# One transformer-like layer on one core: a software pipeline of three attention units instead of two, beside the delta-rule blocks, and one activation table for the normalisations behind it

## The chip, the cores and the metric

The kernel runs on one core of one Trainium2 chip. The metric is the device time of the program in microseconds. All arithmetic is float32 except two small masks.

## What is computed

The layer has DEPTH = 1, 1024 tokens and width 1024. The core of the reference:

```python
p     = x @ w_in
y_A   = rwkv7_time_mix(token_shift(p[:, A]))      # 6 heads x 64, delta-rule state, group norm per head
y_B   = rglru_mix(p[:, B])                        # 4 blocks x 64, gated linear scan
y_C   = stick_breaking_attention(p[:, C])         # 6 heads x 64, strictly causal
x     = layer_norm(ALPHA * x + concat(y_A, y_B, y_C) @ w_out)
x     = layer_norm(ALPHA * x + grouped_moe(x))    # 16 experts, top 2 of one group
...
z         = q @ k.T * scale                       # stick-breaking attention, one query block of 128
log_keep  = where(mask, log_sigmoid(-z), 0)
after     = reversed_cumsum(log_keep) - log_keep
attn      = where(mask, exp(log_sigmoid(z) + after), 0)
o         = head_rms_norm(attn @ v)
```

## The kernel before

**Stages.** TensorE first makes the projections (`proj_pe`, matmuls at L201 and L210), with the gated linear scan and the preparation of the delta rule on the other engines beside it. Then comes the stage that the change touches: 8 delta-rule blocks of 128 tokens (`mats_pe`, `mats_act`, `mats_dve`, `mats_pool`) side by side with the attention. Behind it, in `after_delta_pe`, `after_delta_act` and `after_delta_dve`, come the group norm of the delta rule (six items, `rnorm_*`), the output projection (`out_pe`, L1200), the first LayerNorm (`out_dve`, `out_norm_act`) and the router's logits. The router and the experts (L1677) follow.

**One block of the delta rule** has 13 steps (k = 0 to 12), written as a generator for each engine. Step 0 makes products (L689, L694), which VectorE masks (L811, L816, L805). Step 1 transposes rows (L701), ScalarE copies them (L775). Steps 2 to 10 build an inverse level by level: TensorE multiplies (L640), ScalarE copies a product (L779), VectorE updates two matrices under a mask (L805). Steps 11 and 12 make the block's results (L736, L748 and on), with copies at L795 and L798 and additions at L841 and L842. The state is carried by `state_pe` (L662, L665) and `state_dve` (L674, L675).

**The attention** has 36 units (`SPANS`): a pair of heads, 128 queries and up to 512 keys; 12 units to each pair of heads. A unit goes through: `Z` = q k on TensorE into `PS[0]` (L953, L957), two sigmoids on ScalarE, of -z into `E2` (L1003) and of z (L1007), a reversed running product on VectorE for each head (`sba_scan`, L1021), the weights (`sba_weights`, L1034, with L1031 for a carry), then for each head a transpose on TensorE into the one half of `PS[1]` (L970) and its copy by VectorE (L1043), and the product with v in two halves (L981), which ScalarE copies out (L994). Before the change two units are at work at once: the five pieces (`KINDS`) of number j belong to unit u = j // 5 for the front part and u - 1 for the transposes and the products with v.

**The order** is written out by hand. `side_by_side` runs the generator of a block on each engine, and issues `PIECES[k]` pieces of attention after step k; each engine runs its queue in this order, and semaphores carry the dependences.

```python
PIECES = [3, 2, 1, 2, 1, 2, 1, 2, 1, 2, 2, 2, 2]
for k, _ in enumerate(mats(e, b)):
    if b in SNORM_AT:
        snorm(e, SNORM_AT.index(b), k)
    for _ in range(PIECES[k]):
        piece(e, j)
```

**The head norm of the attention** (`snorm_*`) runs for each pair of heads: a square (L1059), the sum over heads on TensorE (`heads_sum`, L344, into `PS[0]` for the first two pairs), Ln (L1062) and Exp (L1064), and a multiplication on VectorE (L1087). For pairs 0 and 1 it stands in blocks 3 and 6, for pair 2 behind the last block. The next `Z` has to wait until Ln has read `PS[0]`. The tables of ScalarE are loaded where the compiler puts them, unless `exp_ln` (L240) names one that holds both Ln and Exp. The group norm's root is L899 and L901, its use L912, L914 and L917, its means L879 and L906, its gates L884 and L888; the LayerNorm has L1313, L1128 to L1138 on VectorE and L1144, L1146 and L1149 on ScalarE; L1326 transposes for the router, L1340 copies, L1333 makes the logits.

Of the kernel before, what the change touches and what calls it, by code (L numbers as in the profile page):

```python
# [53 lines left out]
def layer_kernel(nc, t, out):  # L54
    ctx = ExitStack()
    with ctx:
# [788 lines left out]

        PIECES = [3, 2, 1, 2, 1, 2, 1, 2, 1, 2, 2, 2, 2]
        KINDS = 5
        SNORM_AT = [3, 6]

        def side_by_side(mats, piece, snorm, e, b):  # L850


            j = b * sum(PIECES)
            for k, _ in enumerate(mats(e, b)):
                if b in SNORM_AT:
                    snorm(e, SNORM_AT.index(b), k)
                for _ in range(PIECES[k]):
                    piece(e, j)
                    j += 1

        def last_pieces(piece, e):

            for j in range(NB * sum(PIECES), KINDS * (NU + 1) + 1):
                piece(e, j)

# [68 lines left out]
        Z, R2 = two(PS[0][:, :]), two(Rl)  # L934
        E2, AT2 = [two(x) for x in Eb], [two(x) for x in ATb]
        carried = [sum(not x[6] for x in SPANS[:u]) for u in range(NU + 1)]
        heads = [(hh, slice(hh * HD, (hh + 1) * HD)) for hh in range(2)]
# [3 lines left out]
        def sba_pe(e, j):  # L941
            u, kind = j // KINDS, j % KINDS
            if kind == 0:
                if u >= NU:
                    return
                n, g, i, lo, hi, first, last = SPANS[u]
                wait(e, s_pe, LRU_T + SBA_T + NT)
                wait(e, s_ba, BA * u)
                wait(e, s_na, z_after_norm[0])
                z_issued[0] = u + 1  # L950
                w = hi - lo
                for hh, h in heads:
                    ins = e.matmul(Z[:, hh, 0:w], SQ[h, g, i * P:(i + 1) * P], SQ[h, 3 + g, lo:hi],  # L953
                                   start=True, stop=not first)
                if first:
                    for hh, h in heads:
                        ins = e.matmul(Z[:, hh, w - P:w], identb[:, :], causal_neg[:, :], start=False, stop=True)  # L957
                ins.then_inc(s_bz, 1)
                return
            u -= 1  # L960
            if not 0 <= u < NU:
                return
            n, g, i, lo, hi, first, last = SPANS[u]
            tiles = range(lo // P, hi // P)
            if kind <= 2:
                hh = kind - 1
                wait(e, s_bd, BD * (u + 1))
                wait(e, s_bt, 2 * u + hh)
                for k in range(len(tiles)):
                    ins = e.transpose(PS[1][:, k * P:(k + 1) * P], E2[u % 2][:, hh, k * P:(k + 1) * P], ident[:, :])  # L970
                ins.then_inc(s_bx, 1)
                return
            cut = (len(tiles) + 1) // 2
            if kind == 3:
                wait(e, s_bt, 2 * u + 2)
                if first:
                    wait(e, s_bo, n)
            ins = None
            for k in (range(cut) if kind == 3 else range(cut, len(tiles))):
                for hh, h in heads:  # L980
                    ins = e.matmul(PS[1][h, HB + (i % 4) * P:HB + (i % 4 + 1) * P],  # L981
                                   SV[:, tiles[k], g * P + hh * HD:g * P + (hh + 1) * HD],
                                   AT2[u % 2][:, hh, k * P:(k + 1) * P], start=first and k == 0,
                                   stop=last and k == len(tiles) - 1)
            if (kind == 4) == (len(tiles) > 1):
                ins.then_inc(s_bv, 1)

        def sba_act(e, j):
            u, kind = j // KINDS, j % KINDS
            if kind == 0:  # L990
                if 2 <= u < NU + 2 and SPANS[u - 2][6]:
                    n, g, i = SPANS[u - 2][0:3]
                    wait(e, s_bv, u - 1)
                    e.copy(YT[:, 5 + g, i * P:(i + 1) * P], PS[1][:, HB + (i % 4) * P:HB + (i % 4 + 1) * P])\  # L994
                     .then_inc(s_bo, 1)
                if u >= NU:
                    return
                w = SPANS[u][4] - SPANS[u][3]
# [5 lines left out]
            if kind == 1 and u < NU:  # L1004
                w = SPANS[u][4] - SPANS[u][3]
                wait(e, s_bv, u - 1)
                e.activation(AT2[u % 2][:, :, 0:w], Z[:, :, 0:w], ACT.Sigmoid).then_inc(s_ba, 1)  # L1007

# [15 lines left out]
        def sba_weights(e, u):  # L1024

            n, g, i, lo, hi, first, last = SPANS[u]
            w = hi - lo
            keep, R = E2[u % 2][:, :, 0:w], R2[:, :, 0:w]
            wait(e, s_bd, BD * u + 2)
            if not last:  # L1030
                e.tensor_tensor(two(carry[:, :]), R[:, :, 0:1], keep[:, :, 0:1], ALU.mult).then_inc(s_bc, 1)  # L1031
                wait(e, s_bc, carried[u + 1])
            wait(e, s_ba, BA * u + 2)
            e.tensor_tensor(keep, AT2[u % 2][:, :, 0:w], R, ALU.mult).then_inc(s_bd, 1)  # L1034

        def sba_dve(e, j):
            u, kind = j // KINDS, j % KINDS
            if kind in (1, 2) and 1 <= u <= NU:
                v, hh = u - 1, kind - 1
                w = SPANS[v][4] - SPANS[v][3]  # L1040
                wait(e, s_bx, 2 * v + hh + 1)
                wait(e, s_bv, v - 1)
                e.tensor_copy(AT2[v % 2][:, hh, 0:w], PS[1][:, 0:w]).then_inc(s_bt, 1)  # L1043
            if u >= NU:
                return
            if kind in (2, 3):
                sba_scan(e, u, kind - 2)
            if kind == 4:
                sba_weights(e, u)
# [4 lines left out]
        def snorm_act(e, g, part):  # L1054
            x, sums = SN[g]
            if part == 0:
                wait(e, s_bo, NT * (g + 1))
                wait(e, s_nd, g)
                e.activation(x, YT[:, 5 + g, :], ACT.Square).then_inc(s_ns, 1)  # L1059
                return  # L1060
            wait(e, s_np, g + 1)
            e.activation(x, sums[:, :], ACT.Ln, scale=1.0 / HD, bias=consts[:, 0:1]).then_inc(s_na, 1)  # L1062
# [3 lines left out]
        def snorm_pe(e, g):  # L1066
# [4 lines left out]
            heads_sum(e, sums, x).then_inc(s_np, 1)  # L1071

        def snorm_pe_at(e, g, k):
            if k == 5:
                snorm_pe(e, g)

        def snorm_act_at(e, g, k):
            if k in (0, 6):
                snorm_act(e, g, k // 6)

        def snorm_dve_at(e, g, k):
            if k == 8:
                snorm_dve(e, g)
# [99 lines left out]
        OUT_KT = [3, 4, 5, 6, 7, 0, 1, 2]  # L1183

        def out_pe(e, i, halves=range(2), kts=OUT_KT):
            for half in halves:
                for kt in kts:
                    if i == 0 and half == 0 and kt == OUT_KT[0]:
                        wait(e, s_ba, BA * NU)
                        wait(e, s_nd, NPAIR)  # L1190
                        wait(e, s_wo, 16 * 4)
                    if i == 0 and half == 0 and kt == 7:
                        wait(e, s_wo2, 16 * 4)
                    if i == 1 and half == 0 and kt == OUT_KT[0]:
# [10 lines left out]
        def after_delta_pe(e):  # L1205
            early, late = OUT_KT[:5], OUT_KT[5:]
            snorm_pe(e, NPAIR - 1)
            for c in range(2):
                state_pe(e, NB - 1, c)
            rnorm_means(e, 0)  # L1210
            rnorm_means(e, 1)
            out_pe(e, 0, [0], early)
            rnorm_gates(e, 0)
            out_pe(e, 0, [1], early)
            rnorm_gates(e, 1)
# [33 lines left out]

        def after_delta_act(e):  # L1250
            snorm_act(e, NPAIR - 1, 0)
            snorm_act(e, NPAIR - 1, 1)
            rnorm_square(e, 0)
# [28 lines left out]
        def after_delta_dve(e):  # L1282
            snorm_dve(e, NPAIR - 1)
            for c in range(2):
# [594 lines left out]
        def _(e):  # L1879
# [5 lines left out]
            for b in range(NB):  # L1885
                side_by_side(mats_act, sba_act, snorm_act_at, e, b)
            last_pieces(sba_act, e)
            after_delta_act(e)
# [7 lines left out]
        def _(e):  # L1896
# [12 lines left out]
            for b in range(NB):  # L1909
                side_by_side(mats_dve, sba_dve, snorm_dve_at, e, b)  # L1910
            last_pieces(sba_dve, e)
            after_delta_dve(e)
# [5 lines left out]
        def _(e):  # L1918
# [4 lines left out]
            for b in range(NB):  # L1923
                side_by_side(mats_pe, sba_pe, snorm_pe_at, e, b)
            last_pieces(sba_pe, e)
            after_delta_pe(e)
# [47 lines left out]
```

## Times and profile before

| | us |
|---|---|
| median of 3 runs (1448.33 to 1450.62) | 1450.27 |
| the profiled execution, its own time | 1446.05 |
| its span | 1444.3 |
| TensorE busy | 1286.6 (89%) |
| VectorE busy | 509.7 (35%) |
| ScalarE busy | 395.9 (27%) |
| GpSimd busy | 103.8 (7%) |
| granted clock of TensorE, mean | 0.955 |

The span goes from the first to the last instruction. Busy shares are means over stages that have different limits, so a change in one stage is read from that stage: the stretch's own busy time, and what ended TensorE's idle time in it. A matmul's duration includes the time until its result is out; back to back they start closer together than they last.

### The profile page before, as it was taken

The page shows a single profiled execution, that of the slowest core. Times are in us where ns is not written, and L with a number is a line of the kernel's source. Part 1 is how long each engine was busy: PE and PEld are TensorE (multiplying, and loading weights), DVE is VectorE, ACT ScalarE, POOL GpSimd, SP SyncE. Part 2 cuts the span into 40 slices and gives each one's busy share as a digit, 9 for nine tenths or more (in the row PEclk, how much of TensorE's full clock was granted, in tenths as well). Part 3 has the DMA queues.
Part 4 walks back from the last instruction along what each step waited for, and adds up shares of the span by engine and source line. Part 5 has one row for each costly group of instructions (what it writes and reads, how often), then busy time and mean ns, then how long its engine had stood idle before and what let it go on. Part 6 is the DMA issues. An engine that isn't in the chain of part 4 may idle for free.

```text
span 1444.3 us, 23140 instructions
## 1 busy us (share of the span) xinstructions
PE 1286.6 (89%) x9639; PEld 642.7 (44%) x9640; DVE 509.7 (35%) x913; ACT 395.9 (27%) x517; POOL 103.8 (7%) x177
## 2 busy tenths in 40 slices
PE   8999999999988888998779993699999999999970
PEld 3444444445666666766434552233333333333320
DVE  3134300444466677676334225311010110101108
ACT  1043302332333343343344333011111111111113
POOL 1000000000111000100000000011101111011110
PEclk9999999999999999999999996799999999999995
DMA  5100101010000000000612203659498498597225
GB/s 204 44 30 29 44 29 44 29 29 0 2 3 3 32 2 18 17 2 2 250 57 86 77 29 145 257 209 347 116 376 302 140 357 309 175 311 273 56 50 226
DMA packets 61012, 170.16 MB, mean 118 GB/s; under 512 B 3184, under 2 KB 3328, under 8 KB 60928
## 3 DMA queue, kind: packets, MB, share of 16 engines
q1 hardware_dynamic: 54384, 145.31, 26.7%
q0 software_dynamic: 6544, 23.62, 6.8%
q8 instruction: 66, 1.08, 0.3%
q14 instruction: 18, 0.15, 0.0%
HBM read 144.28 MB, written 24.64 MB: 117 GB/s over the span
## 4 chain that ended last, share of the span: by engine, by line
PE 81%; DVE 9%; ACT 4%; issue 3%; DMA 2%; SPq 0%; POOL 0%; DVEq 0%; POOLq 0%; ACTq 0%
PE PS L1677 30%; PE PS L201 18%; PE PS L640 6%; PE PS L1200 6%; PE PS L210 3%; PE PS L970 2%; PE PS L981 2%; PE PS L953 2%; PE PS L1670 2%; DVE XS L1043 1%; PE PS L344 1%; PE PS L1333 1%; PE PS L701 1%; DMA XS<-in_xT 1%; DVE XS L816 1%
## 5 line engine op out<-in xcount | busy, mean ns | idle before, releaser
L201 PE MATMUL PS<-XS 128*128 128x512 f32 x672 | 294.6, 597 | 7.1 <-DMA XS<-in_xT 6.6
L1677 PE MATMUL PS<-XS,YT 128*64 128x512 f32 x656 | 286.0, 593 | 0.9 <-DVE YT L1758 0.9
L1677 PE MATMUL PS<-SQ,YT 128*64 128x512 f32 x488 | 214.5, 593 | 0.0
L1677 PE MATMUL PS<-RK,YT 128*64 128x512 f32 x672 | 211.1, 593 | 0.0
L201 PEld LDWEIGHTS PS<-XS 128*128 128x128 f32 x672 | 127.2, 191 | 172.7 <-issue 164.0
L1677 PEld LDWEIGHTS PS<-XS,YT 128*64 128x64 f32 x656 | 88.6, 137 | 181.4 <-issue 180.2
L1200 PE MATMUL PS<-SQ,YT 128*128 128x512 f32 x256 | 116.4, 609 | 4.2 <-DVE YT L917 4.2
L1765 DVE TENSOR_TENSOR YT<-YT,PS 128x256 f32<-128x256 f32 x42 | 15.8, 418 | 270.2 <-PE PS L1677 270.2
L640 PE MATMUL PS<-XS 64*64 64x64 f32 x2880 | 104.8, 225 | 2.1 <-DVE XS L805 1.4
L640 PEld LDWEIGHTS PS<-XS 64*64 64x64 f32 x2880 | 93.7, 139 | 19.2 <-issue 12.3
L1677 PEld LDWEIGHTS PS<-RK,YT 128*64 128x64 f32 x672 | 65.9, 137 | 74.9 <-issue 74.9
L1200 PEld LDWEIGHTS PS<-SQ,YT 128*128 128x128 f32 x256 | 50.0, 198 | 65.7 <-issue 60.1
L1677 PEld LDWEIGHTS PS<-SQ,YT 128*64 128x64 f32 x488 | 66.1, 137 | 0.0
L1778 DVE TENSOR_SCALAR YT<-PS,RK 128x512 f32<-128x512 f32 x21 | 15.8, 751 | 135.5 <-PE PS L1677 135.5
L1043 DVE COPY XS<-PS 128x512 f32<-128x512 f32 (+3 forms) x72 | 40.1, 557 | 55.3 <-PE PS L970 55.0
L970 PE MATMUL PS<-ident,XS 128*128 128x128 f32 x216 | 38.9, 289 | 23.1 <-DVE XS L1043 16.9
L1665 POOL DMA_INDIRECT sums<-YT,RK x21 | 33.6, 1601 | 321.7 <-DVE YT L1778 321.7
L1677 PE MATMUL PS<-YT 128*64 128x512 f32 x120 | 53.6, 593 | 0.0
L1750 ACT ACTIVATE YT<-PS,RK 128x512 f32<-128x512 f32 x21 | 14.4, 687 | 138.2 <-PE PS L1677 138.2
L1744 ACT COPY YT<-PS 128x256 f32<-128x256 f32 x21 | 7.8, 372 | 158.6 <-PE PS L1713 158.6
L981 PE MATMUL PS<-XS,SQ 128*64 128x128 f32 x432 | 36.0, 288 | 15.2 <-DVE XS L1043 15.2
L232 DVE SCALAR_TENSOR_TENSOR RK<-PS,vec,RK 128x1023 f32<-128x1023 f32 x11 | 14.1, 1283 | 97.6 <-ACT RK L221 97.6
(373 smaller groups left out, 1544.0 us busy)
## 6 DMA issues: line engine op xcount, KB each, us to landing
RK<-in_w_down SPq DMA_DIRECT2D x6, 2048.0 KB, 13.1
XS<-in_w_in SPq DMA_DIRECT2D x21, 512.0 KB, 3.2
XS<-in_w_gate SPq DMA_DIRECT2D x5, 2048.0 KB, 12.9
XS<-in_w_upx SPq DMA_DIRECT2D x5, 2048.0 KB, 17.8
XS<-in_w_down SPq DMA_DIRECT2D x5, 2048.0 KB, 10.3
RK<-in_w_gate SPq DMA_DIRECT2D x5, 2048.0 KB, 21.1
SQ<-in_w_gate SPq DMA_DIRECT2D x4, 2048.0 KB, 20.6
RK<-in_w_upx SPq DMA_DIRECT2D x4, 2048.0 KB, 21.8
```

The lines of the kernel that those rows point to most:

```text
L201: m = e.matmul(acc[:, half * HB:(half + 1) * HB], XS[:, 8 + n % 4, kt * P:(kt + 1) * P], XS[:, kt, half * HB:(half + 1) * HB], start=kt == ...
L210: m = e.matmul(acc[:, 0:SBA_W], XS[:, kt, i * P:(i + 1) * P], wv[:, kt, :], start=kt == 0, stop=kt == KT - 1)
L640: ins = e.matmul(block64(acc, r, n), left(r, g, h, n), right(r, g, h, n), start=True, stop=True)
L953: ins = e.matmul(Z[:, hh, 0:w], SQ[h, g, i * P:(i + 1) * P], SQ[h, 3 + g, lo:hi], start=True, stop=not first)
L970: ins = e.transpose(PS[1][:, k * P:(k + 1) * P], E2[u % 2][:, hh, k * P:(k + 1) * P], ident[:, :])
L981: ins = e.matmul(PS[1][h, HB + (i % 4) * P:HB + (i % 4 + 1) * P], SV[:, tiles[k], g * P + hh * HD:g * P + (hh + 1) * HD], AT2[u % 2][:, hh ...
L1043: e.tensor_copy(AT2[v % 2][:, hh, 0:w], PS[1][:, 0:w]).then_inc(s_bt, 1)
L1200: ins = e.matmul(PS[i % 2][:, half * HB:(half + 1) * HB], YT[:, kt, i * P:(i + 1) * P], WO[kt][:, half * HB:(half + 1) * HB], start=kt == ...
L1665: e.indirect_dma_start(sums, bass.IndirectOffsetOnAxis(put_tok, 0), Yb, None, compute_op=ALU.add)\
L1670: ins = e.transpose(PS[1][:, kt * P:(kt + 1) * P], Xg[:, kt * P:(kt + 1) * P], ident[:, :])
L1677: ins = e.matmul(acc[r, :], rows[:, r], third_cols(n, k, at, HB), start=start, stop=stop)
L1765: e.tensor_tensor(Hh[:, f * P:(f + 2) * P], Sg[:, f * P:(f + 2) * P], PS[0][:, HB + f * P:HB + (f + 2) * P], ALU.mult).then_inc(done, 1)
```

## The change

Three units are at work at once. A piece's number gives a step (j % 5), and each engine has its own distance in units for each step, so that between a transpose and its copy's reader stands a step of another unit. The sigmoid of z goes to a buffer of its own. `PIECES` gives 25 pieces to a block instead of 23, so every block begins at the same step (3), and the attention ends within the last block. The third head norm moves into that block (steps 8 to 11), with four matmuls of the output projection (`early_pe`, steps 7 to 10); the sums of the first two norms are made at step 3 instead of 5, and their roots at step 5 instead of 6. `exp_ln` is called ahead of each root of the head norm; nothing switches the table again before the router, so Ln and Exp behind it need no loads.

```diff
-        PIECES = [3, 2, 1, 2, 1, 2, 1, 2, 1, 2, 2, 2, 2]
-        KINDS = 5
-        SNORM_AT = [3, 6]
+        PIECES = [3, 2, 2, 2, 1, 2, 1, 2, 2, 2, 2, 2, 2]
+        KINDS, FIRST = 5, 3
+        SNORM_AT = [3, 6, NB - 1]
...
-            j = b * sum(PIECES)
+            j = FIRST + b * sum(PIECES)
...
+                if b == NB - 1 and early is not None:
+                    early(e, k)
...
+        BETA2 = two(TT[:, 1, :])
...
         def sba_pe(e, j):
-            u, kind = j // KINDS, j % KINDS
-            if kind == 0:
-                if u >= NU:
-                    return
-                n, g, i, lo, hi, first, last = SPANS[u]
+            step = j % KINDS
+            u = j // KINDS - (2, 3, 2, 0, 2)[step]
+            if not 0 <= u < NU:
+                return
+            n, g, i, lo, hi, first, last = SPANS[u]
+            tiles = range(lo // P, hi // P)
+            if step == 3:
...
         def sba_act(e, j):
-            u, kind = j // KINDS, j % KINDS
...
+            step = j % KINDS
+            u = j // KINDS - (3 if step == 2 else 0)
...
+            if step == 4:
+                wait(e, s_bd, BD * u)
+                e.activation(BETA2[:, :, 0:w], Z[:, :, 0:w], ACT.Sigmoid).then_inc(s_ba, 1)
...
         def sba_dve(e, j):
-            u, kind = j // KINDS, j % KINDS
...
+            step = j % KINDS
+            u = j // KINDS - (2, 1, 2, 1, 0)[step]
...
+            exp_ln(e)
             wait(e, s_np, g + 1)
             e.activation(x, sums[:, :], ACT.Ln, scale=1.0 / HD, bias=consts[:, 0:1]).then_inc(s_na, 1)
...
+        SNORM_PE, SNORM_ACT, SNORM_DVE = (3, 3, 9), ((0, 5), (0, 5), (8, 10)), (7, 7, 11)
...
+        def early_pe(e, k):
+
+            if 7 <= k <= 10:
+                out_pe(e, 0, [(k - 7) % 2], [OUT_KT[(k - 7) // 2]])
...
         def after_delta_pe(e):
             early, late = OUT_KT[:5], OUT_KT[5:]
-            snorm_pe(e, NPAIR - 1)
...
-            out_pe(e, 0, [0], early)
+            out_pe(e, 0, [0], early[2:])
             rnorm_gates(e, 0)
-            out_pe(e, 0, [1], early)
+            out_pe(e, 0, [1], early[2:])
...
         def after_delta_act(e):
-            snorm_act(e, NPAIR - 1, 0)
-            snorm_act(e, NPAIR - 1, 1)
```

The head of block 3 on TensorE, before (L970 are transposes, L981 products with v, L953 is `Z`):

```order
L694 MATMUL PS<-RK 64x64 x12
L953 MATMUL PS<-SQ 128x512 x2
L970 MATMUL PS<-ident,XS 128x128 x4
L701 MATMUL PS<-ident,RK 128x128 x2
L701 MATMUL PS<-ident,XS 128x128 x2
```

The same place in the changed kernel, where L965 are the transposes and L975 the products with v:

```order
L953 MATMUL PS<-SQ 128x256 x2
L957 MATMUL PS<-causal_neg,identb 128x128 x2
L975 MATMUL PS<-XS,SQ 64x128 x4
L965 MATMUL PS<-ident,XS 128x128 x4
L701 MATMUL PS<-ident,RK 128x128 x2
L701 MATMUL PS<-ident,XS 128x128 x2
```

Half a product with v now stands ahead of the transposes, which are still ahead of the block's own L701. The head of block 3 on VectorE in the changed kernel (L1028 makes the weights, L1015 is a scan, L1040 a copy of transposed weights):

```order
L816 TENSOR_TENSOR XS<-PS,mask 128x3x4x64 x2
L805 COPY_PREDICATED XS<-upper,XS 128x384
L1028 TENSOR_TENSOR XS<-TT 128x1024
L1011 MEMSET TT 128x1
L1015 SCALAR_TENSOR_TENSOR TT<-XS 128x255
L1040 COPY XS<-PS 128x512
```

The weights that the transposes read are behind the block's masks, as they were before. ScalarE in block 3 around the head norm, before:

```order
L779 COPY XS<-PS 128x384
L1062 ACT_TABLE_LOAD
L1062 ACTIVATE TT<-PS,consts 128x1024
L1064 ACT_TABLE_LOAD
L1064 ACTIVATE TT<-TT 128x1024
L994 COPY YT<-PS 128x128
L1003 ACT_TABLE_LOAD
L1003 ACTIVATE XS<-PS 128x2x384
```

And in the changed kernel (L242 is the table of Ln and Exp, L1058 Ln, L1060 Exp, L998 and L1001 the two sigmoids):

```order
L779 COPY XS<-PS 128x384
L242 ACT_TABLE_LOAD
L1058 ACTIVATE TT<-PS,consts 128x1024
L1060 ACTIVATE TT<-TT 128x1024
L998 ACT_TABLE_LOAD
L998 ACTIVATE XS<-PS 128x1024
L1001 ACTIVATE TT<-PS 128x1024
```

One load less; the copy ahead of the first load is now that of step 5's product (L779), which is the instruction that TensorE issues right before the `Z` that waits for Ln. Before, a product with v and a whole level (L981, L640) stood between the sums (L344) and that `Z`.

## Rows read from the trace of the kernel before

**Rows 1.** The page's first line.

```profile
span 1444.3 us, 23140 instructions
```

**Rows 2.** Busy time by stretch: us, PE, PEld, DVE, ACT, POOL (x count), PEclk, DMA share, GB/s.

```profile
373.10:705.75 332.65, 282.15 (x5940) 221.12 (x5935) 225.01 (x427) 129.77 (x203) 32.24 (x48) 0.97 0.05 16
705.75:791.95 86.20, 76.45 (x164) 33.23 (x165) 31.46 (x44) 39.99 (x45) 2.06 (x28) 0.93 0.33 123
791.95:887.00 95.05, 82.50 (x321) 49.82 (x319) 28.79 (x40) 29.30 (x34) 0.00 (x0) 0.90 0.14 57
```

**Rows 3.** Waits from 373 to 706 us: who waited for whom, us in total, times, longest.

```profile
PE PS L970 <- DVE XS L1043: 16.9, 15, 3.2
PE PS L981 <- DVE XS L1043: 15.2, 18, 3.1
PE PS L970 <- DVE XS L1034: 6.0, 5, 3.4
PE PS L662 <- DVE RK L675: 4.7, 1, 4.7
```

**Rows 4.** TensorE at the head of blocks: start, us, instruction, [idle before <- releaser].

```profile
415.57 0.55 PE L970 MATMUL PS<-ident,XS 128*128 128x128 f32 x3 [0.82 <-DVE XS L1034]
...
452.88 0.63 PE L970 MATMUL PS<-ident,XS 128*128 128x128 f32 x4 [3.24 <-DVE XS L1043]
...
494.96 0.66 PE L970 MATMUL PS<-ident,XS 128*128 128x128 f32 x4 [3.41 <-DVE XS L1034]
...
537.91 1.09 PE L981 MATMUL PS<-XS,SQ 128*64 128x128 f32 x16 [3.15 <-DVE XS L1043]
...
577.39 0.40 PE L970 MATMUL PS<-ident,XS 128*128 128x128 f32 x1 [2.10 <-DVE XS L1043]
...
657.26 0.66 PE L970 MATMUL PS<-ident,XS 128*128 128x128 f32 x2 [3.19 <-DVE XS L1043]
```

**Rows 5.** VectorE in block 3: masks, weights, and a scan.

```profile
491.16 1.82 DVE L816 TENSOR_TENSOR XS<-PS,mask 128x768 f32<-128x768 f32 x2
...
493.68 1.22 DVE L1034 TENSOR_TENSOR XS<-XS,TT 128x1024 f32<-128x1024 f32 x1
...
526.78 1.27 DVE L1021 TENSOR_TENSOR_SCAN TT<-XS,carry 128x511 f32<-128x511 f32 x1
```

**Rows 6.** TensorE, `Z` at the head of block 3.

```profile
490.42 1.13 PE L953 MATMUL PS<-SQ 64*128 64x512 f32 x4
```

**Rows 7.** ScalarE, the head norm in block 3.

```profile
510.02 0.48 ACT L779 COPY XS<-PS 128x384 f32<-128x384 f32 x1 [3.05 <-PE PS L640]
...
511.92 1.11 ACT L1062 ACTIVATE TT<-PS,consts 128x1024 f32<-128x1024 f32 x1
513.06 1.28 ACT L1064 ACT_TABLE_LOAD   x1
514.35 1.06 ACT L1064 ACTIVATE TT<-TT 128x1024 f32<-128x1024 f32 x1
```

**Rows 8.** TensorE behind the last block; the first is the page's group of L1200.

```profile
L1200 PE MATMUL PS<-SQ,YT 128*128 128x512 f32 x256 | 116.4, 609 | 4.2 <-DVE YT L917 4.2
```

**Rows 9.** TensorE's timeline behind the last block.

```profile
705.75 3.78 PE L879 MATMUL PS<-RK,head_ones 128*128 128x512 f32 x4 [0.71 <-DVE RK L675]
...
738.37 6.85 PE L1200 MATMUL PS<-SQ,YT 128*128 128x512 f32 x12 [4.23 <-DVE YT L917]
...
758.46 2.07 PE L884 MATMUL PS<-RK,g_up 128*128 128x512 f32 x2 [5.52 <-DVE RK L906]
```

**Rows 10.** VectorE before the last of these waits.

```profile
752.78 1.23 DVE L1138 TENSOR_TENSOR RK<-RK,TT 128x1024 f32<-128x1024 f32 x1
...
755.54 0.75 DVE L912 SCALAR_TENSOR_TENSOR RK<-RK,vec,TT 128x512 f32<-128x512 f32 x1 [1.54 <-ACT TT L901]
```

**Rows 11.** TensorE, two waits in the router's part.

```profile
801.72 2.70 PE L1333 MATMUL PS<-RK,TT 128*128 128x16 f32 x16 [1.86 <-ACT TT L1340]
...
879.18 1.97 PE L1326 MATMUL PS<-ident,RK 128*128 128x128 f32 x8 [8.42 <-DVE RK L1138]
```

More of the change, by code:

```diff
@@ L844, in mats_dve, with side_by_side @@
             yield
-        PIECES = [3, 2, 1, 2, 1, 2, 1, 2, 1, 2, 2, 2, 2]
-        KINDS = 5
-        SNORM_AT = [3, 6]
-        def side_by_side(mats, piece, snorm, e, b):
-            j = b * sum(PIECES)
+        PIECES = [3, 2, 2, 2, 1, 2, 1, 2, 2, 2, 2, 2, 2]
+        KINDS, FIRST = 5, 3
+        SNORM_AT = [3, 6, NB - 1]
+        def side_by_side(mats, piece, snorm, early, e, b):
+            j = FIRST + b * sum(PIECES)
             for k, _ in enumerate(mats(e, b)):
@@ L859, in side_by_side @@
                     j += 1
-        def last_pieces(piece, e):
-            for j in range(NB * sum(PIECES), KINDS * (NU + 1) + 1):
-                piece(e, j)
+                if b == NB - 1 and early is not None:
+                    early(e, k)
         ITEMS = [(half, g) for half in range(2) for g in range(NPAIR)]
@@ L959, in sba_pe @@
                 return
[L960 to L966, printed above, removed]
+            if step in (0, 2):
+                hh = step // 2
                 wait(e, s_bd, BD * (u + 1))
@@ L972, in sba_pe @@
                 return
-            cut = (len(tiles) + 1) // 2
-            if kind == 3:
+            half = (len(tiles) + 1) // 2
+            if step == 4:
                 wait(e, s_bt, 2 * u + 2)
@@ L977, in sba_pe @@
                     wait(e, s_bo, n)
-            ins = None
-            for k in (range(cut) if kind == 3 else range(cut, len(tiles))):
+            for k in (range(half) if step == 4 else range(half, len(tiles))):
                 for hh, h in heads:
@@ L984, in sba_pe @@
                                    stop=last and k == len(tiles) - 1)
-            if (kind == 4) == (len(tiles) > 1):
+            if (step == 1) == (len(tiles) > 1):
                 ins.then_inc(s_bv, 1)
         def sba_act(e, j):
-            u, kind = j // KINDS, j % KINDS
[L990 to L998, printed above, removed]
+            step = j % KINDS
+            u = j // KINDS - (3 if step == 2 else 0)
+            if not 0 <= u < NU:
+                return
+            n, g, i, lo, hi, first, last = SPANS[u]
+            w = hi - lo
+            if step == 2 and last:
+                wait(e, s_bv, u + 1)
+                e.copy(YT[:, 5 + g, i * P:(i + 1) * P], PS[1][:, HB + (i % 4) * P:HB + (i % 4 + 1) * P])\
+                 .then_inc(s_bo, 1)
+            if step == 3:
                 wait(e, s_bz, u + 1)
@@ L1003, in sba_act @@
                 e.activation(E2[u % 2][:, :, 0:w], Z[:, :, 0:w], ACT.Sigmoid, scale=-1.0).then_inc(s_ba, 1)
[L1004 to L1007, printed above, removed]
+            if step == 4:
+                wait(e, s_bd, BD * u)
+                e.activation(BETA2[:, :, 0:w], Z[:, :, 0:w], ACT.Sigmoid).then_inc(s_ba, 1)
         def sba_scan(e, u, hh):
@@ L1033, in sba_weights @@
             wait(e, s_ba, BA * u + 2)
-            e.tensor_tensor(keep, AT2[u % 2][:, :, 0:w], R, ALU.mult).then_inc(s_bd, 1)
+            e.tensor_tensor(keep, BETA2[:, :, 0:w], R, ALU.mult).then_inc(s_bd, 1)
         def sba_dve(e, j):
-            u, kind = j // KINDS, j % KINDS
[L1038 to L1044, printed above, removed]
-                return
-            if kind in (2, 3):
-                sba_scan(e, u, kind - 2)
-            if kind == 4:
+            step = j % KINDS
+            u = j // KINDS - (2, 1, 2, 1, 0)[step]
+            if not 0 <= u < NU:
+                return
+            if step in (0, 2):
+                hh = step // 2
+                w = SPANS[u][4] - SPANS[u][3]
+                wait(e, s_bx, 2 * u + hh + 1)
+                wait(e, s_bv, u - 1)
+                e.tensor_copy(AT2[u % 2][:, hh, 0:w], PS[1][:, 0:w]).then_inc(s_bt, 1)
+            if step in (1, 4):
+                sba_scan(e, u, step % 4)
+            if step == 3:
                 sba_weights(e, u)
@@ L1071, in snorm_pe @@
             heads_sum(e, sums, x).then_inc(s_np, 1)
+        SNORM_PE, SNORM_ACT, SNORM_DVE = (3, 3, 9), ((0, 5), (0, 5), (8, 10)), (7, 7, 11)
         def snorm_pe_at(e, g, k):
-            if k == 5:
+            if k == SNORM_PE[g]:
                 snorm_pe(e, g)
         def snorm_act_at(e, g, k):
-            if k in (0, 6):
-                snorm_act(e, g, k // 6)
+            if k in SNORM_ACT[g]:
+                snorm_act(e, g, SNORM_ACT[g].index(k))
         def snorm_dve_at(e, g, k):
-            if k == 8:
+            if k == SNORM_DVE[g]:
                 snorm_dve(e, g)
@@ L1189, in out_pe @@
                         wait(e, s_ba, BA * NU)
-                        wait(e, s_nd, NPAIR)
+                        wait(e, s_nd, NPAIR - 1)
                         wait(e, s_wo, 16 * 4)
                     if i == 0 and half == 0 and kt == 7:
+                        wait(e, s_nd, NPAIR)
                         wait(e, s_wo2, 16 * 4)
@@ L1282, in after_delta_dve @@
         def after_delta_dve(e):
-            snorm_dve(e, NPAIR - 1)
             for c in range(2):
@@ L1885, in _ @@
             for b in range(NB):
-                side_by_side(mats_act, sba_act, snorm_act_at, e, b)
-            last_pieces(sba_act, e)
+                side_by_side(mats_act, sba_act, snorm_act_at, None, e, b)
             after_delta_act(e)
@@ L1909, in _ @@
             for b in range(NB):
-                side_by_side(mats_dve, sba_dve, snorm_dve_at, e, b)
-            last_pieces(sba_dve, e)
+                side_by_side(mats_dve, sba_dve, snorm_dve_at, None, e, b)
             after_delta_dve(e)
@@ L1923, in _ @@
             for b in range(NB):
-                side_by_side(mats_pe, sba_pe, snorm_pe_at, e, b)
-            last_pieces(sba_pe, e)
+                side_by_side(mats_pe, sba_pe, snorm_pe_at, early_pe, e, b)
             after_delta_pe(e)
```

## The prediction

> **What bounds the kernel now.** I read the page's first line for the size of the whole [rows 1], then busy time by stretch, and cut the program where the change ends: the eight blocks with the attention up to the first mean of the group norm (373.1 to 705.75), the group norm with the first output tiles (to 791.95), the rest up to the router (to 887) [rows 2]. The reader should see TensorE busy for 282.15 of 332.65, 76.45 of 86.2 and 82.5 of 95.05 us. VectorE has 225 of 332.65 in the first. So TensorE bounds each of them, and a reordering can win at most its idle time: 50.5, 9.75 and 12.55 us, plus what a fuller clock gives (0.97, 0.93, 0.90 granted). The experts behind 887 are not touched and should only shift.
>
> The waits of the first stretch [rows 3] say who ends the 50.5 us: transposes and products with v that wait for L1043's copy or for the weights, 16.9 + 15.2 + 6.0 = 38.1 us in 38 places, and one of 4.7. These are two kinds. At the head of six blocks the wait is long [rows 4]: 0.82 + 3.24 + 3.41 + 3.15 + 2.10 + 3.19 = 15.9 us. There VectorE makes the block's masks, and attention waits behind them. The other 22.2 us are 32 short round trips through a copy, some 0.7 each.
>
> **The change, part by part.** The number of TensorE instructions stays, and so does its work of 282 us, but for 3.4 us that come into the stretch (below). I count idle time.
>
> *Short round trips: 22.2 us go.* A transpose and its reader now have another unit's piece or a level of the inverse between them. A copy of 512 takes about as long as such a step.
>
> *Heads of blocks: 15.9 become 18.7.* Every block now begins at step 3, with `Z`, half a product with v, and transposes. The order on VectorE puts the weights for these transposes behind the masks. From the start of `Z` at 490.42 [rows 6] to where VectorE is free for the weights, 493.5, is 3.1 us; 493.68 in this trace had a carry ahead of it. Weights of 512 keys take 1.22 [rows 5]. TensorE has `Z` (1.06 of its slot in 1.13) and half a product (0.5; the 16 records of the whole take 1.09 [rows 4]) to do. So a head with all widths 512 waits 3.1 + 1.2 - 1.6 = 2.7. With the widths of the units at the seven heads (5, 10, 15 and on) I get 3.0, 3.3, 3.1, 2.4, 1.9, 2.9 and 2.1, sum 18.7. Two heads that had little or no wait now have one.
>
> *New seams: 8 us.* Where ScalarE has two sigmoids ahead of the copy of a level (steps 3 and 9), where the last piece of a block is a product of a narrow unit, which has no second half, and where the copy at L795 is waited for, I walked three blocks with durations of this trace and found 0.2 to 0.8 us a place, some 1.3 a block over six blocks.
>
> *The first two head norms: 8.4 us.* In blocks 3 and 6 TensorE issues step 5's product and then `Z`, which waits for Ln. ScalarE first copies that product (0.48), then loads the table (1.28) and runs Ln (1.11) [rows 7]. That is 2.9 and the hops, 3.1 us of idle TensorE each, where the trace of before has none: there the load was done ahead. The scan behind that `Z` is late as well, since Exp (1.06) and the sigmoid's load (1.28) come first, and an update of the inverse stands behind the scan: 1.1 more. Twice 4.2. One load of 1.28 fewer in each norm wins nothing, as it is the last of the three that stays.
>
> *First and last block: 7 us.* The first has few pieces, about 4. In the last, the third norm and four matmuls of the output projection lie beside levels; the wait of 4.7 [rows 3] at the state goes, because VectorE no longer has the norm's multiplication ahead of the state. What stays is 3.
>
> Idle time after: 18.7 + 8 + 8.4 + 7 = 42, against 50.5. The stretch loses 8.5 and gains the four matmuls, two records each at 116.4 / 256 = 0.455 or 0.43 [rows 8] at the full clock: +3.4.
>
> *Group norm.* -3.4 for these four. The wait of 4.23 [rows 9] comes behind Ln, load, Exp: -1.28. That of 5.52 has three loads in its chain; without them VectorE's L1138 becomes the last. It ends 1.28 sooner, at 752.7 instead of 754.0, and L912 follows it rather than 755.54 [rows 10]: -2.8. The four records of L879 took 3.78 where 4 x 0.43 is 1.8 [rows 9], at half the clock behind the wait of 4.7: -2.0. Sum -9.5.
>
> *To the router.* The last tile's norm has two loads in the open ahead of the wait of 8.42: -2.6. The wait of 1.86 for L1340, which ScalarE runs behind the same norm of an earlier tile, goes [rows 11]: -1.9. Sum -4.5.
>
> *Clock.* The two new waits of 3 us will each be followed by matmuls at the lower level about every other time, at 2 us a time: +2.
>
> Sum: -8.5 + 3.4 - 9.5 - 4.5 + 2 = -17. The profiled execution took 1446.05; it becomes 1429. The median of the runs, 1450.27, stands 4.2 above it and should become 1433.
>
> **A rule that speaks about the loads.** The trace shows Ln ending at 513.03, the load from 513.06 to 514.34, Exp from 514.35 [rows 7]: a switch costs 1.28 and nothing else. The Trainium skill (ScalarE: Activation LUTs, "What ACT_TABLE_LOAD costs") counts a drain of 1380 ns on top, 2.66 us a switch; no drain is seen here. By that page the six loads counted above would be worth 8 us more.
>
> **Rivals.**
>
> *A, the new waits are covered* (0.2). The seams vanish and VectorE comes early to the weights, so that only heads and first and last block stay, 26 us idle; the clock keeps its higher level behind the group norm's shorter waits (L1200's 12 records took 6.85 where 12 x 0.43 is 5.2, and as much again at L884). -24.5 + 3.4 - 9.5 - 4.5 - 3.7 = -39: 1411. For it: I added hops, and VectorE is busy only two thirds of the stretch. Against: its queue is in order.
>
> *B, slower* (0.06). On VectorE a scan (1.27 for 512 [rows 5]) now stands right ahead of an update of the inverse at four levels of a block, and it waits for a sigmoid of a `Z` that was issued a moment ago. If each of the 28 updates in seven blocks comes late by a whole scan, that is 35.6 us, in place of the seams and the norms' share, 11: 1433 + 25 = 1458. It decides from 1.0 us an update on. Against: my walk finds it late by 0 to 0.6, as TensorE still has transposes to do.
>
> *C, the gain goes back* (0.05). The transposes' waits move to the heads and norms in full, the stretch's idle time is 57 to 60 instead of 42, and the matmuls there fall to the lower clock more often: what the group norm gains is used up, 1448 to 1453. Here the change doesn't do what it says: the steps between transpose and reader exist, and something else is late next.
>
> *D, each removed switch is worth another 1.28* (0.03), as an engine that empties before it would show: six in the open, -7.7: 1425. The gaps of 0.03 and 0.01 beside the load [rows 7] speak against it. This is what the page's rule comes to.
>
> **How the numbers follow.** My forecast's own case has 0.66: 1418 to 1446. A measurement of this kernel can tell some 0.2%, 3 us, from no change. The predicted time is 1433. The range goes from case A's end to the edge of C: 1412 to 1447; B, most of C and a tail below A lie outside. Faster: 0.63 of the forecast's case, A, D and a little of C, 0.87. Same: 0.03 of the forecast's and 0.03 of C, 0.06. Slower: B and the rest of C, 0.07.
>
> **What would show it.** In the profile after: the short waits of transposes and products for L1040's copy under 5 us in total; at the head of blocks 1 to 7 a wait of 1.9 to 3.3 us of L965 for L1028; in blocks 3 and 6 a wait of `Z` for L1058 of 3 us; no table load between the last norm's and the router; TensorE's idle time up to the first mean near 42 us. Wrong would be: no such wait of `Z`, idle time near 26 or above 55 us, or an L640 that waits for L805 by more than 1 us in most levels.

## The result and the profile after

| | before | changed |
|---|---|---|
| median, us | 1449.8 (4 runs) | 1415.26 (4 runs, 1412.85 to 1417.94) |
| span of the profiled execution | 1444.3 | 1412.6 |
| TensorE busy | 1286.6 | 1278.6 |
| ScalarE busy | 395.9 | 356.0 |

The ratio is 0.9773, 95% interval 0.9758 to 0.9787. The change saves 34.5 us, twice what I had forecast (17). It lies near the lower end of the range (1412), and outside the 1418 to 1446 of the forecast's own case: 1415.26 is 4 us from rival A's end (1411) and 18 from my 1433. The spans of the two profiled executions differ by 31.7, less than the medians, because the one of the kernel before (1446.05) was quicker than its median.

The stretches of rows 2, cut at the same instructions (first mean of the group norm, first transpose for the router, router). Busy time by stretch of the changed kernel, columns as in [rows 2] (the third cut as the row of before under it):

```profile
373.10:692.29 319.19, 284.31 (x5944) 220.13 (x5937) 223.21 (x427) 125.91 (x200) 33.83 (x48) 0.98 0.06 22
692.29:768.83 76.54, 70.99 (x157) 30.71 (x158) 32.73 (x45) 16.68 (x27) 2.06 (x28) 0.96 0.34 127
...
768.80:854.70 85.90, 78.93 (x321) 47.69 (x319) 26.64 (x35) 16.32 (x23) 0.00 (x0) 0.95 0.14 57
```

And of the kernel before, the third stretch cut at the router's first addition on VectorE, L1408, as above:

```profile
792.00:885.90 93.90, 82.45 (x321) 49.78 (x319) 27.89 (x38) 29.15 (x33) 0.00 (x0) 0.90 0.15 57
```

Idle is the stretch's length less TensorE's busy time:

| stretch | length, us | idle | busy |
|---|---|---|---|
| blocks and attention | 332.65 to 319.19, -13.5 | 50.5 to 34.9, -15.6 | 282.2 to 284.3, +2.1 |
| group norm | 86.20 to 76.54, -9.7 | 9.75 to 5.55, -4.2 | 76.45 to 70.99, -5.5 |
| to the router | 93.9 to 85.9, -8.0 | 11.45 to 6.97, -4.5 | 82.45 to 78.93, -3.5 |

The four early matmuls (3.4 us) are work that went from the second stretch to the first. The sum is 31.2 us of the 31.7 by which the spans differ; the experts only shift.

TensorE's waits in the first stretch of the changed kernel, to be laid beside [rows 3] (who waited for whom, us in total, times, longest):

```profile
PE PS L965 <- DVE XS L1028: 17.1, 7, 3.0
...
PE PS L953 <- ACT TT L1058: 6.2, 2, 3.1
...
PE PS L640 <- ACT XS L779: 2.6, 5, 1.3
...
PE PS L640 <- DVE XS L805: 2.0, 2, 1.6
PE PS L701 <- DVE XS L816: 1.9, 1, 1.9
...
PE PS L662 <- DVE RK L675: 1.0, 1, 1.0
...
PE PS L689 <- ACT XS L798: 1.0, 3, 0.4
...
PE PS L344 <- ACT TT L1001: 0.3, 1, 0.3
...
PE PS L965 <- DVE XS L1040: 0.2, 1, 0.2
```

The round trips through a copy are gone: 0.2 us where L970 and L981 had waited 22.2 outside the heads. The heads of blocks are all there, seven waits of transposes for the weights, 17.1 us. And there is a wait that the kernel before did not have, `Z` for Ln of the head norm, 3.1 us in blocks 3 and 6.

ScalarE around the head norm in block 3, beside [rows 7]:

```profile
509.52 0.48 ACT L779 COPY XS<-PS 128x384 f32<-128x384 f32 x1 [3.19 <-PE PS L640]
510.02 1.28 ACT L242 ACT_TABLE_LOAD   x1
511.31 1.11 ACT L1058 ACTIVATE TT<-PS,consts 128x1024 f32<-128x1024 f32 x1
512.46 1.06 ACT L1060 ACTIVATE TT<-TT 128x1024 f32<-128x1024 f32 x1
513.53 1.28 ACT L998 ACT_TABLE_LOAD   x1
```

TensorE there:

```profile
508.56 0.92 PE L640 MATMUL PS<-XS 64*64 64x64 f32 x24
512.57 1.13 PE L953 MATMUL PS<-SQ 64*128 64x512 f32 x4 [3.10 <-ACT TT L1058]
...
517.70 0.92 PE L640 MATMUL PS<-XS 64*64 64x64 f32 x24 [1.60 <-DVE XS L805]
```

The chain is the one forecast: product, copy, load, Ln, and only then `Z`. The scan behind waits as well, and with it the update that L640 needs (1.60).

Behind the last block, beside [rows 9]:

```profile
692.29 1.98 PE L876 MATMUL PS<-RK,head_ones 128*128 128x512 f32 x4 [0.71 <-DVE RK L675]
...
717.82 7.11 PE L1204 MATMUL PS<-SQ,YT 128*128 128x512 f32 x12 [2.94 <-DVE YT L914]
...
735.27 1.13 PE L881 MATMUL PS<-RK,g_up 128*128 128x512 f32 x2 [2.61 <-DVE RK L903]
```

The four means take 1.98 instead of 3.78 us, since the wait ahead of the state is 1.0 and not 4.7. The waits of 4.23 and 5.52 have become 2.94 and 2.61.

### The profile page after: what moved, and what is told of

Its sections match the earlier page's. It is cut to its first block, busy times and chain, and to the rows that moved or that the text cites. A ratio compares the mean times of both kernels' runs of the same rounds, so it can differ in the third digit from the quotient of the medians.

```text
span 1412.6 us, 23110 instructions
## 1 busy us (share of the span) xinstructions
PE 1278.6 (91%) x9639; PEld 637.0 (45%) x9640; DVE 507.8 (36%) x913; ACT 356.0 (25%) x486; POOL 105.3 (7%) x177
## 4 chain that ended last, share of the span: by engine, by line
PE 83%; DVE 8%; ACT 4%; issue 3%; DMA 2%; SPq 0%; POOL 0%; DVEq 0%; POOLq 0%; ACTq 0%
PE PS L1677 31%; PE PS L201 18%; PE PS L1204 7%; PE PS L640 6%; PE PS L210 3%; PE PS L965 2%; PE PS L1670 2%; PE PS L975 2%; PE PS L953 2%; PE PS L344 1%; PE PS L701 1%; PE PS L1333 1%; DVE XS L816 1%; PE PS L736 1%; DMA XS<-in_xT 1%
## 5 line engine op out<-in xcount | busy, mean ns | idle before, releaser
L640 PE MATMUL PS<-XS 64*64 64x64 f32 x2880 | 104.2, 225 | 5.2 <-ACT XS L779 2.6
L640 PEld LDWEIGHTS PS<-XS 64*64 64x64 f32 x2880 | 93.1, 138 | 21.9 <-issue 12.4
L1204 PEld LDWEIGHTS PS<-SQ,YT 128*128 128x128 f32 x256 | 48.8, 194 | 62.3 <-issue 58.3
L965 PE MATMUL PS<-ident,XS 128*128 128x128 f32 x216 | 39.2, 290 | 17.4 <-DVE XS L1028 17.1
L1040 DVE COPY XS<-PS 128x512 f32<-128x512 f32 (+3 forms) x72 | 39.5, 549 | 27.4 <-PE PS L965 27.2
L998 ACT ACTIVATE XS<-PS 128x1024 f32<-128x1024 f32 (+3 forms) x36 | 29.2, 811 | 66.2 <-PE PS L957 44.2
```

What stands on the lines that cost most here:

```text
L640: ins = e.matmul(block64(acc, r, n), left(r, g, h, n), right(r, g, h, n), start=True, stop=True)
L1040: e.tensor_copy(AT2[u % 2][:, hh, 0:w], PS[1][:, 0:w]).then_inc(s_bt, 1)
L1204: ins = e.matmul(PS[i % 2][:, half * HB:(half + 1) * HB], YT[:, kt, i * P:(i + 1) * P], WO[kt][:, half * HB:(half + 1) * HB], start=kt == ...
```

## The experiments

The times of the kernel before beside each group of runs were 1451.03 (the first four), 1448.34 (the next three) and 1448.63 us (the last two).

### The table alone

```diff
                 return
+            exp_ln(e)
             wait(e, s_np, g + 1)
```

in the kernel before.

> The kernel before with exp_ln ahead of each root of the head norm, and nothing else. My theory, that the table is worth what its loads cost on the chains in the open: 1.3 us in front of the state behind the last block, 4.1 in the group norm, 4.5 before the router, and up to 3.4 more where the clock stays at its upper level at the router's first logits: 10 to 13 us, so 1437 to 1440, with TensorE's idle time before the first mean still near 49 us. Rival, that the table alone is worth little and the units carry the gain: 1445 or more. Rival, that each switch costs another 1.28 us that the trace does not show: 1430 or less.

1434.53 us (ratio 0.9885, 0.9866 to 0.9904): 16.5 us for one line, between the first theory and the last. The trace of the kernel before has 74 table loads, this one 43, the changed kernel 43 as well: 31 loads fewer, which at 1.28 us make 39.7 of the 39.9 us by which ScalarE's busy time fell (395.9 to 356.0). The three stretches of this run:

```profile
373.10:708.40 335.30, 286.50 (x5936) 224.60 (x5928) 224.67 (x427) 125.87 (x200) 32.42 (x48) 0.95 0.05 16
708.40:789.80 81.40, 75.80 (x165) 33.01 (x166) 32.72 (x45) 16.66 (x27) 2.06 (x28) 0.94 0.36 137
789.80:875.70 85.90, 78.89 (x321) 47.67 (x319) 26.63 (x36) 16.32 (x23) 0.00 (x0) 0.94 0.14 56
```

The group norm is 4.8 shorter (4.1 expected, and 4.15 of the 4.8 is idle time), the stretch to the router 8.0, to the tenth what the whole change has there. Of these 8.0, 4.4 are idle time, the two chains of loads that I had priced, and 3.6 is busy time with the same instructions: the clock. Granted clock at the router's first logits, before (801 to 809) and in this run (798 to 806):

```profile
801.00:809.00 8.00, 7.28 (x28) 5.63 (x29) 2.25 (x2) 1.68 (x2) 0.00 (x0) 0.61 0.36 131
```

```profile
798.00:806.00 8.00, 8.00 (x35) 4.80 (x35) 0.00 (x0) 1.01 (x1) 0.00 (x0) 1.00 0.38 131
```

Before, TensorE had waited 1.86 us for L1340 [rows 11] and then ran at the lower level (1.2 GHz) for most of these 8 us; without the wait it stays at 2.4 GHz. This comes back in every profile here: TensorE is busy for 82.5 us of this stretch in the three traces that have the wait (before, its second profile, the units alone), and for 78.9 in all others. The first stretch is longer here than before, 335.3, with 1.7 us less idle time (48.8) and 4.3 more busy. So the profiled executions show 10.2 us up to the router, and the medians 16.5. Which executions were profiled makes the rest: that of before took 1446.05, 5.0 less than the median beside this run (1451.03), and this one 1436.17, 1.6 more than its own. Against the second profile of the kernel before (the last runs below) the three stretches are 14.7 shorter.

### The units alone

```diff
-            exp_ln(e)
             wait(e, s_np, g + 1)
```

in the changed kernel. "The units" stands here for all of the change but the table: the third unit, the 25 pieces, the norm in the last block and the four early matmuls. No run takes these apart but the one with the norm behind the block.

> The changed kernel without exp_ln in the head norm, so that the loads stand where they stood before. If the two parts add up: the change's 34.5 us less the 10 to 13 of the table, so 1425 to 1428; idle time of TensorE before the first mean near 35 us. If the units' part is only the 3 to 8 us that I forecast for the stretch: 1430 or more beside a table that is worth over 20. The waits of Z for Ln in blocks 3 and 6 stay at 3.1 us.

1437.35 us (0.9905, 0.9882 to 0.9927), with a spread of 9 us, 1430.06 to 1439.17. The medians of the two halves give 16.5 + 13.7 = 30.2 against 34.5 of the whole; with intervals of 2 to 3 us on each, the gap of 4.3 isn't clear of noise. Idle time adds up much better. Its first stretch:

```profile
373.10:699.90 326.80, 290.58 (x5940) 224.81 (x5929) 223.29 (x427) 129.82 (x203) 33.70 (x48) 0.95 0.06 20
```

36.2 us idle: the units take away 14.3 of 50.5, the table 1.7, together 16.0 where the whole has 15.6. Busy time is 290.6 against 284.3 of the changed kernel, at 0.95 against 0.98 of the clock. So no wait is missing that one part opens and the other closes, and in the profiled execution the difference is clock. The time lay above the 1425 to 1428 expected, mostly since the table's half was worth 16.5 and not 10 to 13.

### Both roots one step earlier

```diff
-        SNORM_PE, SNORM_ACT, SNORM_DVE = (3, 3, 9), ((0, 5), (0, 5), (8, 10)), (7, 7, 11)
+        SNORM_PE, SNORM_ACT, SNORM_DVE = (3, 3, 9), ((0, 4), (0, 4), (8, 10)), (7, 7, 11)
```

> The changed kernel with the roots of the first two head norms at step 4 instead of 5 on ScalarE, ahead of the copy of step 5's product. My theory: load and Ln then run beside the level of step 4, both waits of Z for Ln (3.1 us each) and the 1.6 us of L640 for L805 behind the first go, 7.8 us, and nothing takes their place: 1407 to 1409. Rival: the copy L779 now stands behind Exp and the sigmoid's work, and the wait moves to L640 or the scan: 1412 to 1415.

1412.13 us (0.9736, 0.9718 to 0.9754). ScalarE in block 3:

```profile
503.80 1.28 ACT L242 ACT_TABLE_LOAD   x1
505.51 1.11 ACT L1058 ACTIVATE TT<-PS,consts 128x1024 f32<-128x1024 f32 x1 [0.43 <-PE PS L344]
```

One of its waits, and its first stretch:

```profile
PE PS L640 <- DVE XS L805: 2.8, 3, 1.3
```

```profile
373.10:685.30 312.20, 282.77 (x5948) 218.87 (x5948) 223.11 (x427) 125.78 (x200) 33.93 (x48) 0.98 0.07 21
```

The load is over before the sums are there, and the list of waits has no L953 any more: 6.2 us gone. But L640 still waits for L805, 2.8 us where it was 2.0, so idle time falls by 5.5 (34.9 to 29.4) and not by 7.8. The stretch takes 312.2 instead of 319.2 us. Of these 7.0 the profiled execution kept 2.2 to its end: 1.7 went to a lower clock in the group norm (0.93 against 0.96), and 3.1 behind the router, where it took 561.0 against 557.9 us. The changed kernel's own two profiles take 557.9 and 561.3 there, so these 3.1 say nothing of the edit. The median moved by 3.1, and by 5 if each is taken by its ratio to the kernel before beside it. That the waits of `Z` go is shown. The time, 1412.13, is short of the 1407 to 1409 expected and is that of the rival (1412 to 1415), of whose mechanism the trace has the 0.8 us more of L640.

### Blocks that begin at step 1

```diff
-        KINDS, FIRST = 5, 3
+        KINDS, FIRST = 5, 1
...
-        SNORM_PE, SNORM_ACT, SNORM_DVE = (3, 3, 9), ((0, 5), (0, 5), (8, 10)), (7, 7, 11)
+        SNORM_PE, SNORM_ACT, SNORM_DVE = (4, 4, 9), ((0, 4), (0, 4), (9, 10)), (7, 7, 11)
```

> The changed kernel with every block beginning at step 1 instead of 3 (FIRST = 1), so that the pieces at a block's head need nothing that VectorE has behind the masks; the roots as in the run before, the sums at step 4, the last norm's square at step 9. My theory: the seven waits at the heads (17.1 us) shrink to under 5 in total, some 3 come back elsewhere, since every other step meets another level: 1395 to 1400. Rival, that VectorE's 3 us of masks must be waited for by somebody in order: the transposes behind the head wait instead, and it is 1406 to 1409, the gain of the roots alone. Rival on the other side: a scan falls ahead of an update of the inverse at more places: above 1415.

1394.38 us (0.9616, 0.9596 to 0.9636), 21 us below the changed kernel and the best here. Its waits and its first stretch:

```profile
PE PS L965 <- DVE XS L1028: 2.9, 4, 1.1
PE PS L736 <- DVE XS L805: 2.6, 4, 0.7
...
PE PS L701 <- DVE XS L816: 2.4, 3, 1.9
...
PE PS L975 <- DVE XS L1040: 2.0, 4, 0.7
```

```profile
373.10:671.40 298.30, 279.19 (x5945) 215.13 (x5936) 224.50 (x427) 125.32 (x200) 38.64 (x48) 1.00 0.07 23
```

17.1 us of transposes for weights have become 2.9, and idle time is 19.1. The clock is at 1.00, and the same instructions are busy for 279.2 us instead of 284.3. So what stood behind the masks did not have to be there: with the order turned by two steps, the head has transposes of weights made long before, and `Z`.

### Blocks that begin at step 4

```diff
-        KINDS, FIRST = 5, 3
+        KINDS, FIRST = 5, -1
...
-        SNORM_PE, SNORM_ACT, SNORM_DVE = (3, 3, 9), ((0, 5), (0, 5), (8, 10)), (7, 7, 11)
+        SNORM_PE, SNORM_ACT, SNORM_DVE = (6, 6, 10), ((0, 6), (0, 6), (10, 11)), (8, 8, 12)
```

> As the kernel whose blocks begin at step 1, but with FIRST = -1, so that every block begins at step 4 (a product, then the transposes of a unit whose weights VectorE made before the masks); sums and roots of the first two norms at step 6, the third norm at steps 10 to 12. If what costs at the heads is only that the weights stand behind the masks, this start wins as well: the seven waits under 5 us in total, 1393 to 1401. If step 1 won by luck of the places where steps and levels meet: 1406 or more.

1395.36 us (0.9636, 0.9619 to 0.9654), the same as from step 1 within the spread. Its longest waits are others:

```profile
PE PS L965 <- DVE XS L1040: 6.2, 7, 1.6
PE PS L701 <- DVE XS L816: 5.4, 6, 2.5
...
PE PS L965 <- DVE XS L1028: 0.8, 1, 0.8
```

```profile
373.10:672.10 299.00, 280.76 (x5944) 216.35 (x5936) 226.05 (x427) 125.64 (x200) 32.73 (x48) 0.99 0.05 18
```

The transposes wait for L1028 once, 0.8 us, and idle time is 18.2. Some waiting for the masks and for a copy is left, 11.6 us. What the two starts have in common is that no transpose at the head needs weights made behind the masks, and they win the same. Against the run with the roots at step 4 (1412.13) that is 17 to 18 us by the medians, 15 to 17 by the ratios. The idle time saved is 10 to 11 of it (29.4 to 19.1 and 18.2), since other waits came in place of some of the 17.1; the rest is a fuller clock and the spread between executions. The cause of the waits at the heads, weights made behind the masks, is shown.

### Matmuls that fill the heads

```diff
-                wait(e, s_bd, BD * (u + 1))
                 wait(e, s_bt, 2 * u + hh)
+                if (j - FIRST) % sum(PIECES) == 2:
+                    keep_clock(e, PS[1][:, 0:HB], 8)
+                wait(e, s_bd, BD * (u + 1))
```

The added matmuls write to the bank that the transposes overwrite.

> The changed kernel with eight more bf16 matmuls of 128x512 ahead of the transposes at each block's head, into the bank that the transposes will write: TensorE is busy in most of the wait for the weights, which stays as long as it was. It tells what the clock has to do with the heads. If the fall of the clock follows the waits, the stretch's clock rises from 0.98 to 1.00 but for blocks 3 and 6, and 2 to 4 us go: 1411 to 1413. If the waits cost only their own time: 1414 to 1417. If the added matmuls outlast the waits: above 1417.

1411.31 us (0.9751, 0.9737 to 0.9766), 3 to 4 us under the changed kernel and within the 1411 to 1413 expected if the clock's fall follows the waits. But the intervals overlap (0.9758 to 0.9787 and 0.9745 to 0.9786 for the changed kernel), so the gain is not clear of noise. TensorE at the head of block 1, and the first stretch:

```profile
412.42 1.67 PE L634 MATMUL PS<-restart,identb 128*128 128x512 bf16 x7 [0.16 <-issue]
415.03 0.55 PE L967 MATMUL PS<-ident,XS 128*128 128x128 f32 x3 [0.93 <-DVE XS L1030]
```

```profile
373.10:689.70 316.60, 293.45 (x5998) 222.98 (x6004) 223.23 (x427) 125.96 (x200) 34.02 (x48) 0.99 0.06 21
```

The transposes still start when the weights are there; the wait as such is filled, not shortened. The clock of the stretch is 0.99, against 0.98 and 0.97 in the two profiles of the changed kernel, and the stretch is 2.6 and 4.7 us shorter. That the waits at the heads cost some clock fits this; how much, this run doesn't settle.

### The third norm behind the block again

```diff
-        SNORM_AT = [3, 6, NB - 1]
+        SNORM_AT = [3, 6]
...
         def after_delta_pe(e):
             early, late = OUT_KT[:5], OUT_KT[5:]
+            snorm_pe(e, NPAIR - 1)
...
-            out_pe(e, 0, [0], early[2:])
+            out_pe(e, 0, [0], early)
```

and likewise on the other engines, with no `early_pe`.

> The changed kernel with the third head norm and the four early matmuls behind the last block again, as before the change; the rest stays. My theory of the tail: VectorE again has the norm's multiplication ahead of the state, so L662's wait of 1.0 us becomes some 3 (4.7 in the kernel before, less one table load), the sums wait 1 to 1.5 us for the square, and three levels of the last block have nothing beside them, some 0.8 us each: 5 to 8 us slower than the changed kernel, 1420 to 1423. Rival, that the tail only moves the same work and the chain of the last block sets the end anyway: within 2 us of it, 1413 to 1417.

1424.37 us (0.9839, 0.9825 to 0.9853), 9 above the changed kernel. Behind the last block:

```profile
690.62 3.32 PE L344 MATMUL PS<-TT,head_ones 128*128 128x512 f32 x4 [1.88 <-ACT TT L1054]
698.18 0.91 PE L662 MATMUL PS<-XS 64*64 64x64 f32 x12 [3.10 <-DVE RK L675]
700.44 3.78 PE L876 MATMUL PS<-RK,head_ones 128*128 128x512 f32 x4 [0.71 <-DVE RK L675]
```

Two of the three waits expected are there, 3.1 us at the state and 1.9 at the sums; the third, levels of the last block with nothing beside them, is one wait of 0.8 (L736 for L805) and 0.6 more of L640 for L779, not three of 0.8. Idle time to the first mean rises by 3.5 us only, to 38.4. The rest is clock: busy time in the first stretch is 288.9 with 3.4 us less work in it, and the means take 3.78 us again. The time is above the 1420 to 1423 expected, and the profiled execution (1428.26) was the slowest of the five.

### Both kernels again

No edit; a second profile of each.

> The changed kernel again, for a second profiled execution. If its idle time before the first mean is a matter of the order alone, it comes out at 35 us within 1 us, and the waits at the heads at 17 us; if the clock's falls differ from one execution to the next, TensorE's busy time in that stretch differs by some us (284.3 in the first) with the same instructions. Time 1412 to 1418.

> The kernel before again, likewise: idle 50.5 us within 1 us before the first mean, busy time 282.2 in the first profile, now anywhere from 279 to 289. Time 1446 to 1452.

1415.89 and 1448.22 us. The first stretch of each again, cut at the first mean:

| | first profile: idle, busy | second: idle, busy |
|---|---|---|
| before | 50.5, 282.2 | 50.49, 286.21 |
| changed | 34.9, 284.3 | 34.88, 286.42 |

Idle time comes back to 0.02 us. Busy time differs by 2 to 4 us with the same instructions. So a table of waits can be trusted to a tenth, and a sum over a stretch only to some 4 us. From 373.1 to the router the second pair differs by 35.6 us where the first has 31.2; the 34.5 of the medians lies between.

## Why the forecast held, and why it was half the size

The range held because it took in rival A's side. The forecast's own case, 1418 to 1446, missed the time, though its waits came as described, and A, which set the lower end, did not come as described. So the range held in part by luck. What failed is the size of two terms.

**Bound and kind of gain: right.** TensorE bounds all three stretches, and idle time and clock are all that was won.

**Short round trips, 22.2 us: right.** 0.2 are left for the copy.

**Heads, 18.7: right in kind, 1.6 too high.** 17.1 in seven waits. I had 3.0, 3.3, 3.1, 2.4, 1.9, 2.9, 2.1 and the trace shows 2.76, 3.04, 2.82, 2.28, 1.60, 2.60 and 2.02.

**Head norms, 8.4: right.** Twice 3.10 and once 1.60, 7.8. The run with the roots at step 4 took the two of 3.10 away. I had the late update twice, and it came once: in block 6 no L640 waits for L805.

**First and last block, 7: right,** about 6.5: 3.8 in the first (1.9 of L701, 1.3 of L640 for L779, 0.4 and 0.2) and 2.6 in the last (0.9, 1.0 and 0.7). The run with the norm behind the block shows what it had cost.

**New seams, 8 us: this step failed.** They are 2.6: outside the first and the last block L640 waits 1.3 us for L779, L689 1.0 for L798 and L344 0.3 for L1001. I had walked the blocks, with some 0.25 us for the hop from a matmul's end to its reader and 0.1 back. The trace has 0.05 each way. TensorE and ScalarE of the changed kernel in block 5:

```profile
582.16 1.13 PE L953 MATMUL PS<-SQ 64*128 64x512 f32 x4
583.22 0.44 PE L975 MATMUL PS<-XS,SQ 128*64 128x128 f32 x4
...
585.70 1.61 PE L640 MATMUL PS<-XS 64*64 64x64 f32 x48 [0.61 <-ACT XS L779]
```

```profile
583.34 1.02 ACT L998 ACTIVATE XS<-PS 128x1024 f32<-128x1024 f32 x1 [0.58 <-PE PS L953]
584.26 1.02 ACT L1001 ACTIVATE TT<-PS 128x1024 f32<-128x1024 f32 x1
585.16 0.49 ACT L779 COPY XS<-PS 128x384 f32<-128x384 f32 x1
```

`Z` (L953) ends at 583.29 and the first sigmoid starts at 583.34; the copy ends at 585.65 and its reader starts at 585.70. This is a seam of the kind that I had counted, two sigmoids ahead of a copy, at 0.2 to 0.8 a place; it is 0.61. That hops of 0.2 too much account for all of the 5.4 us is argued, not shown: the prediction gives neither the hops nor the single places, and durations in my walk may have been off too.

**Clock, +2: this step failed as well.** I had priced only new waits of 3 us. At the router's logits 3.5 us were won where a wait of 1.86 went; I had the wait in the sum and put the clock behind it at nothing. In the first stretch, with the added 3.4 us of work set aside, busy time fell by 1.3 us in one pair of profiles and 3.2 in the other, where I had a rise of 2; that is within the spread of 2 to 4 us. A wait's length doesn't tell whether the clock falls: in the kernel before it was 0.58 from 577 to 580 us, behind the wait of 2.10 [rows 4], and 1.00 from 538 to 544, behind that of 3.15.

**Group norm, -9.5: right,** -9.7. **To the router, -4.5:** 4.5 of idle time, and the 3.5 of clock.

Together: seams 5.4, heads 1.6, norms and ends 1.1, less 0.9 us of idle time that stands in no term, make 7.2 of idle time (42.1 forecast, 34.9 measured). With 3.3 of clock in the first stretch (this pair of profiles), 3.5 at the router and 0.2 in the group norm that is 14.2; 17 forecast and these are 31.2, the sum of the three stretches.

**Rivals.** A, at 1411, is the nearest in time: the seams were covered and the clock was kept in places. But its idle time of 26 us is not what the trace shows (34.9), since the waits of `Z` stayed. B did not come: L640 waits for L805 twice, 2.0 us. C did not come either. D, another 1.28 a switch, has no place in the stretches: the table's part of the idle time, 1.7 + 4.1 + 4.4 us, is near what I priced with loads of 1.28 alone (1.3 in the expectation of that run, 4.1 and 4.5). The Trainium skill's rule on what a load costs (ScalarE: Activation LUTs, "What ACT_TABLE_LOAD costs") counts a drain of 1380 ns beside the load. The trace disagrees: in the changed kernel a load runs from 510.02 to 511.30 and Ln starts at 511.31.

## What to carry to other kernels

Where two streams of work share in-order queues, look at what stands at the one place where a long piece of the one stream meets the other: turning the phase of the same pieces by two steps was worth 18 us here (1412.13 to 1394.38), more than the units alone (13.7), though only 10 us of the 18 is idle time. A function sequence that one table can hold should name that table; one line gave 16 us, since loads stood on the way from a sum to the matmul that waited for its result. And in a sum over hand-walked steps, take the hop between engines from rows as well: the seams, walked with hops of up to 0.25 us where the trace has 0.05, came out 5.4 us too dear, a third of what this forecast missed.

## What was not expected of the hardware

Idle time of TensorE over 6000 instructions repeats to 0.02 us between executions, while busy time of the same instructions varies by 2 to 4 us with the granted clock. A wait of 1.86 us was followed by most of 8 us at the lower clock level (granted clock 0.61), which makes a short wait cost three times its length; the same place without the wait had 1.00. The kernel before had 0.61 there again in its second profile (805.5 to 813.5). The whole first stretch ran at 1.00 in the run whose blocks begin at step 1, where its longest wait was 1.9 us, and at 0.99 in the one from step 4, where it was 2.5. And the 31 table loads that one line removed, 39.7 us of ScalarE's time, were worth 10.3 us of TensorE's idle time, since it waited behind only a few of them.
